# Attention in a hybrid encoder step: where VectorE combines the preceding tile, for tiles wider than 512 columns

## The chip, the cores and the metric

One core of a Trainium2 chip runs the whole step as one program. The metric is the device time of one execution in microseconds (us), lower is better. The median of three runs stands for the kernel; beside it there is one profiled execution with a trace of every instruction.

## The reference: what is computed

One layer of a streaming encoder: a modulated norm, an input projection, two mixers side by side (a state-space group and a differential-attention group), an output projection, and a gated convolutional feed-forward part. A prompt of 1,024 rows and eight samples of 16 rows (each with a cache of 512 keys) go through it. The change touches differential attention alone:

```python
def diff_attention(q, k, v, qpos, kpos, lam, rel_bias):
    s = jnp.einsum('bqhmd,bkhmd->bhmqk', q, k) * (DA_DK ** -0.5)       # m: two maps
    ...
    visible = (kpos[None, :] // CHUNK) <= (qpos[:, None] // CHUNK)
    p = jax.nn.softmax(jnp.where(visible, s + bias, -jnp.inf), axis=-1)
    attn = p[:, :, 0] - lam * p[:, :, 1]
    return jnp.einsum('bhqk,bkhd->bqhd', attn, v)
```

Each of four heads has two maps: two score matrices, each with a softmax of its own. The second is taken off the first with a factor, and the difference weighs the values.

## The kernel before, in words

**Tiles.** The prompt's attention is 32 tiles (4 heads, 8 blocks of 128 query rows). Block i sees (i + 1) x 128 key columns, so that its width is 128 to 1,024. In each head the blocks come in the order 7, 0, 6, 1, 5, 2, 4, 3 (`TILE_ORDER`), so blocks 7, 6, 5 and 4 are the ones wider than 512 columns (1,024, 896, 768 and 640). "Block 7" below is the tile of that block in some head; heads count from 0. The eight samples' tiles stand between them: ahead of the prompt tiles number 5, 9, 13, 17, 21, 25, 28 and 31 (`SAMPLE_BEHIND`). The list of the 40 is `WORK`, and w is a place in it.

**Work of one tile, over three engines.** TensorE (PE) makes the scores of both maps (L985). For each map VectorE (DVE) adds the bias to the last 256 columns (L1551) and takes the negated row maximum (L1552, `row_max`). ScalarE (ACT) makes the exponentials of that map and their sums (L2058). When both maps have theirs, VectorE combines them: a reciprocal (L1570), a factor (L1571), and one pass over the width that writes `attn` (L1576). This is `combine`; a sample's is `combine_s` (L1582 to L1591). TensorE turns `attn` in blocks of 128 (L650), in one piece of up to four blocks or, for a wide tile, in two pieces, ScalarE copies each piece out of PSUM (L2087, `attn_T`), and TensorE multiplies with the values (L1046); ScalarE copies the product into `o_T` (L2104). TensorE also turns the samples' cached keys (L650 with `k_cache`), and ScalarE copies them (L2074).

**Order.** Every engine runs a list that is written out by hand, step by step over w, and waits on semaphores. In step w VectorE did the two maxima of tile w and then combined tile w - 1. TensorE and ScalarE do this:

```python
# TensorE, step w (L1063)
scores(w)
attn_turn(w - 2, 0)
attn_values(w - 3)            # waits for ScalarE's last copy of tile w - 3
attn_turn(w - 2, 1)           # only where tile w - 2 is wide
# ScalarE, step w (L2106)
turn_out(w - 2, 0)
o_out(w - 3)
exps(w)                       # map 0, then map 1: each waits for its row maximum
turn_out(w - 2, 1)            # only where tile w - 2 is wide
```

(The two lists are shortened: the key turns and their copies stand ahead of `scores` and `turn_out`, and samples have functions of their own.) Two PSUM banks take turns for everything that TensorE turns and for the products with the values, so each use also waits until ScalarE has emptied the use two before it (`aux_free`).

Of the kernel before, what the change touches and what calls it, by code (L numbers as in the profile page):

```python
# [78 lines left out]
def build(nc, a, o):  # L79
# [231 lines left out]
    with ctx:  # L311
# [4 lines left out]
        def sem(name):  # L316
            if name not in sems:
                sems[name] = ctx.enter_context(nc.semaphore(name))
            return sems[name]
# [9 lines left out]
        def mark(ins, name):  # L329

            count[name] = count.get(name, 0) + 1
            ins.then_inc(sem(name), 1)
# [30 lines left out]
        def up_done(grp, u):  # L363

            if grp:
                return NUP0 + u + 1
            return max(i for i, (v, _) in enumerate(UP_ORDER) if v == u) + 1
# [5 lines left out]
        for i in range(LEAD, 2 * FT):  # L373
            for _ in range(2 if i == FT else 1):
                MIXED.append(("u", 1, sum(k == "u" for k, _, _ in MIXED)))
            MIXED.append(("d", 0, i))
        for i in range(FT):
            for _ in range(2 if i == 0 else 1):
                if sum(k == "u" for k, _, _ in MIXED) < 2 * FT:
                    MIXED.append(("u", 1, sum(k == "u" for k, _, _ in MIXED)))  # L380
            MIXED.append(("d", 1, i))
# [101 lines left out]
        WORK = []  # L483
# [3 lines left out]
        NW = len(WORK)  # L487
# [3 lines left out]
        def tile_width(w):  # L491

            kind, t = WORK[w]
            return (PROMPT[t][1] + 1) * P if kind == "p" else PAST + TS
# [15 lines left out]
        def score_bank(w, m):  # L510

            return 2 * PAIRS[w][m] if len(PAIRS[w]) == 2 else 2 * PAIRS[w][0] + m
# [41 lines left out]
        def aux_bank(of):  # L554

            return 6 + USE[of] % 2
# [654 lines left out]
        def _(ve):  # L1211
            def ch(ins):
                step(ve, ins, "dve_step")
# [143 lines left out]
            for c in range(8):  # L1357
# [11 lines left out]
                for t in range(4):  # L1369
                    w = SSMC[:, c, t:t + 1]  # L1370
# [168 lines left out]

            PSF = PS[:, :, :].rearrange("p b n -> p (b n)")  # L1540

            def row_max(w):
                t = WORK[w][1]
                W = tile_width(w)
                for m in range(2):
                    ve.wait_ge(sem("scores"), 2 * t + m + 1)
                    if t >= 2:
                        ve.wait_ge(sem("exp"), EXPS[PROMPT_AT[t - 2]][1])
                    c0 = 512 * score_bank(w, m)
                    near = PSF[:, c0 + max(0, W - 2 * P):c0 + W]  # L1550
                    ch(ve.tensor_tensor(near, near, BIASP[:, PROMPT[t][0], 2 * P - min(W, 2 * P):], ALU.add))  # L1551
                    mark(ve.tensor_reduce(MX[:, 2 * (t % 2) + m:2 * (t % 2) + m + 1], PSF[:, c0:c0 + W], AX.X,  # L1552
                                          ALU.max, negate=True), "row_max")
# [39 lines left out]
            def o_rows(w):  # L1593
                b = WORK[w][1]
                ve.wait_ge(sem("aux"), USE["values", w, 0] + 1)
                if b >= 1:
                    nxt = ("turn", w, 0)
                    ve.wait_ge(sem("aux"), USE[nxt] + 1)
                mark(ve.tensor_copy(OB[:, :], PS[:, aux_bank(("values", w, 0)), 0:P]), "o_rows")

            for w in range(NW + 3):
                if w < NW:
                    (row_max if WORK[w][0] == "p" else row_max_s)(w)
                if 1 <= w < NW + 1:
                    (combine if WORK[w - 1][0] == "p" else combine_s)(w - 1)
                if w == NW:
                    mark(ve.memset(EL[:, NH * NPT:], 0.0), "dve_step")
                    ch(ve.tensor_tensor(EL[:, 0:NH * NPT], L1[:, :], L1[:, :], ALU.mult))
                    ch(ve.tensor_scalar(EL[:, 0:NH * NPT], EL[:, 0:NH * NPT], -1.0, DV * EPS, ALU.add, ALU.mult))
                if w >= 3 and WORK[w - 3][0] == "s":  # L1610
                    o_rows(w - 3)
# [933 lines left out]
```

## Time and profile before

| | before |
|---|---|
| median of 3 runs | 1695.97 us (1694.97 to 1696.41) |
| the profiled execution | 1696.15 us, span 1694.4 us |
| PE busy over the span | 1593.2 us (94%) |
| DVE / ACT / POOL busy | 994.3 (59%) / 651.8 (38%) / 453.6 us (27%) |
| attention, 519 to 690 us of the span: PE / DVE / ACT busy | 144.9 / 123.9 / 105.9 us of 171 |

The profiled execution's time is its span and 1.75 us around it. Busy times are sums over instructions, and PE's ends are modelled. Attention is the stretch of the span from 519 to 690 us; there no engine is busy all the time, which is to say that each waits for the others in turn.

### The profile page before, as it was taken

The page shows a single profiled execution, that of the slowest core. Times are in us where ns is not written, and L with a number is a line of the kernel's source. Part 1 is how long each engine was busy: PE and PEld are TensorE (multiplying, and loading weights), DVE is VectorE, ACT ScalarE, POOL GpSimd, SP SyncE. Part 2 cuts the span into 40 slices and gives each one's busy share as a digit, 9 for nine tenths or more (in the row PEclk, how much of TensorE's full clock was granted, in tenths as well). Part 3 has the DMA queues.
Part 4 walks back from the last instruction along what each step waited for, and adds up shares of the span by engine and source line. Part 5 has one row for each costly group of instructions (what it writes and reads, how often), then busy time and mean ns, then how long its engine had stood idle before and what let it go on. Part 6 is the DMA issues. An engine that isn't in the chain of part 4 may idle for free.

```text
span 1694.4 us, 23175 instructions
## 1 busy us (share of the span) xinstructions
PE 1593.2 (94%) x9153; PEld 1412.9 (83%) x9153; DVE 994.3 (59%) x1603; ACT 651.8 (38%) x1143; POOL 453.6 (27%) x274
## 2 busy tenths in 40 slices
PE   4899998899998888789999999999999999999996
PEld 3689897689996666668899999999889989989875
DVE  3765416732115777654776666666466687667834
ACT  4531223321114666644332232224444454445532
POOL 0121124332201000365743333333621121112232
PEclk8899999899999999999999999999999999999998
DMA  9545110231214222327522222222364435544442
GB/s 326 198 163 199 38 28 1 57 89 38 67 53 155 101 101 77 124 87 205 203 68 67 66 62 63 63 78 73 99 188 124 133 103 167 160 135 122 149 164 70
DMA packets 163858, 189.09 MB, mean 112 GB/s; under 512 B 7851, under 2 KB 126868, under 8 KB 163731
## 3 DMA queue, kind: packets, MB, share of 16 engines
q1 hardware_dynamic: 148074, 148.89, 28.1%
q10 hardware_dynamic: 10300, 21.01, 4.1%
q0 software_dynamic: 5376, 17.71, 3.0%
q8 instruction: 73, 1.20, 0.3%
q14 instruction: 35, 0.28, 0.1%
HBM read 170.48 MB, written 17.11 MB: 111 GB/s over the span
## 4 chain that ended last, share of the span: by engine, by line
PE 81%; DVE 10%; ACT 3%; issue 3%; DMA 2%; POOL 1%; ACTq 0%; DVEq 0%; SPq 0%; POOLq 0%
PE PS L727 17%; PE PS L728 16%; PE PS L729 16%; PE PS L1188 4%; PE PS L1190 4%; PE PS L1189 4%; PE PS L650 4%; PE PS L1117 2%; PE PS L1118 2%; PE PS L1119 2%; PE PS L1046 2%; PE PS L985 2%; DVE y_new L1666 1%; PE PS L740 1%; DMA weights_raw<-in_w_up_dram 1%
## 5 line engine op out<-in xcount | busy, mean ns | idle before, releaser
L2347 POOL TENSOR_TENSOR weights_lo<-weights_raw,weights_hi 128x1024 fp32r<-128x1024 f32 x103 | 267.6, 2601 | 696.4 <-ACT weights_hi L1876 532.3
L727 PE MATMUL PS<-h_hi,weights_hi 128*128 128x384 f32 x1280 | 433.9, 339 | 3.3 <-DVE h_lo L1279 2.9
L728 PE MATMUL PS<-h_lo,weights_hi 128*128 128x384 f32 x1280 | 431.4, 337 | 0.0
L729 PE MATMUL PS<-h_hi,weights_lo 128*128 128x384 f32 x1280 | 431.3, 337 | 0.0
L1876 ACT ACTIVATE weights_hi<-weights_raw 128x1024 fp32r<-128x1024 f32 x202 | 213.2, 1058 | 159.1 <-PE PS L1190 97.5
L727 PEld LDWEIGHTS PS<-h_hi,weights_hi 128*128 128x128 f32 x1280 | 241.7, 189 | 11.9 <-issue 11.7
L728 PEld LDWEIGHTS PS<-h_lo,weights_hi 128*128 128x128 f32 x1280 | 241.7, 189 | 0.1
L729 PEld LDWEIGHTS PS<-h_hi,weights_lo 128*128 128x128 f32 x1280 | 241.6, 189 | 0.0
L1188 PE MATMUL PS<-weights_hi,g_hi 128*128 128x512 f32 x396 | 159.3, 402 | 8.9 <-POOL g_lo L2485 5.5
L1190 PE MATMUL PS<-weights_hi,g_lo 128*128 128x512 f32 x396 | 157.4, 397 | 0.0
L1189 PE MATMUL PS<-weights_lo,g_hi 128*128 128x512 f32 x396 | 156.6, 396 | 0.0
L2485 POOL TENSOR_TENSOR g_lo<-g_T,g_hi 128x384 fp32r<-128x384 f32 x54 | 70.4, 1305 | 271.5 <-ACT g_hi L2232 271.5
L1822 DVE TENSOR_TENSOR weights_lo<-weights_raw,weights_hi 128x1024 fp32r<-128x1024 f32 x99 | 121.7, 1256 | 21.2 <-ACT weights_hi L1876 18.6
L727 PE MATMUL PS<-h_hi_b,weights_hi 128*128 128x384 f32 x352 | 118.4, 336 | 0.2 <-DVE weights_lo L1822 0.2
L729 PE MATMUL PS<-h_hi_b,weights_lo 128*128 128x384 f32 x352 | 118.1, 336 | 0.0
L728 PE MATMUL PS<-h_lo_b,weights_hi 128*128 128x384 f32 x352 | 118.1, 336 | 0.0
L1188 PEld LDWEIGHTS PS<-weights_hi,g_hi 128*128 128x128 f32 x396 | 74.8, 189 | 26.4 <-DVE weights_lo L1822 7.9
L1190 PEld LDWEIGHTS PS<-weights_hi,g_lo 128*128 128x128 f32 x396 | 74.8, 189 | 18.6
L1189 PEld LDWEIGHTS PS<-weights_lo,g_hi 128*128 128x128 f32 x396 | 74.9, 189 | 15.7
L1733 DVE SCALAR_TENSOR_TENSOR beside_h_hi<-up_val,ffn_conv_cols,beside_h_hi 128x768 f32<-128x768 f32 x44 | 83.8, 1904 | 1.6
L1733 DVE SCALAR_TENSOR_TENSOR beside_h_hi<-up_gate,ffn_conv_cols,beside_h_hi 128x768 f32<-128x768 f32 x44 | 83.3, 1894 | 1.5
L2256 ACT ACTIVATE up_val<-PS 128x384 f32<-128x384 f32 x44 | 21.7, 492 | 138.1 <-PE PS L729 138.1
(389 smaller groups left out, 2465.3 us busy)
## 6 DMA issues: line engine op xcount, KB each, us to landing
weights_raw<-in_w_up_dram SPq DMA_DIRECT2D x88, 512.0 KB, 3.9
weights_raw<-in_w_down_dram SPq DMA_DIRECT2D x66, 512.0 KB, 4.4
w_ada_unit<-in_w_ada_dram SPq DMA_DIRECT2D x32, 512.0 KB, 5.4
weights_raw<-in_w_in_dram SPq DMA_DIRECT2D x24, 512.0 KB, 5.4
weights_raw<-in_w_out_dram SPq DMA_DIRECT2D x24, 512.0 KB, 4.0
w_ada<-in_w_ada_dram SPq DMA_DIRECT2D x4, 2048.0 KB, 16.7
k_cache<-in_cache_k_dram SPq DMA_DIRECT2D x8, 1024.0 KB, 7.7
v_cache<-in_cache_v_dram SPq DMA_DIRECT2D x8, 1024.0 KB, 5.5
```

The lines of the kernel that those rows point to most:

```text
L650: return pe.transpose(out, src, C("ident", rows, 0, rows))
L727: pe.matmul(out, wh, xh, start=(i == 0), stop=False)
L728: pe.matmul(out, wh, xl, start=False, stop=False)
L729: mm = pe.matmul(out, wl, xh, start=False, stop=(i == n - 1))
L1188: pe.matmul(out, GH[i % 2][:, lhs], WH[n % 3][:, ws], start=(f == 0), stop=False)
L1189: pe.matmul(out, GH[i % 2][:, lhs], WL[n % 3][:, ws], start=False, stop=False)
L1190: mm = pe.matmul(out, GL[i % 2][:, lhs], WH[n % 3][:, ws], start=False, stop=(f == FT - 1))
L1733: ins = ve.scalar_tensor_tensor(out=d, in0=src, scalar=w, in1=d, op0=ALU.mult, op1=ALU.add)
L1822: mark(ve.tensor_tensor(WL[n % 3][:, :], WR[:, n % 3, :], WH[n % 3][:, :].bitcast(F32), ALU.subtract), "w_lo_dve")
L1876: mark(ac.activation(WH[n % 3][:, :], WR[:, n % 3, :], ACT.Copy), "w_hi")
L2347: mark(gp.tensor_tensor(WL[n % 3][:, :], WR[:, n % 3, :], WH[n % 3][:, :].bitcast(F32), ALU.subtract), "w_lo")
L2485: mark(gp.tensor_tensor(GL[i % 2][:, :], GT[f][:, gg, :], GH[i % 2][:, :].bitcast(F32), ALU.subtract), "g_lo")
```

## The change

For a prompt tile w that is wider than 512 columns (and w at least 1), VectorE does the maximum of map 0, combines the tile before it, and then does the maximum of map 1. For all other tiles the order stays: both maxima, then the combination. Four wide tiles in each of four heads less the very first tile make 15 steps. No instruction is added or taken away, and the lists of the other engines stay as they were.

```diff
-            def row_max(w):
+            def row_max(w, maps=(0, 1)):
                 t = WORK[w][1]
                 W = tile_width(w)
-                for m in range(2):
+                for m in maps:
...
+            def combined(w):
+                (combine if WORK[w][0] == "p" else combine_s)(w)
+
             for w in range(NW + 3):
-                if w < NW:
-                    (row_max if WORK[w][0] == "p" else row_max_s)(w)
-                if 1 <= w < NW + 1:
-                    (combine if WORK[w - 1][0] == "p" else combine_s)(w - 1)
+                if 1 <= w < NW and WORK[w][0] == "p" and tile_width(w) > 512:
+                    row_max(w, (0,))
+                    combined(w - 1)
+                    row_max(w, (1,))
+                else:
+                    if w < NW:
+                        (row_max if WORK[w][0] == "p" else row_max_s)(w)
+                    if 1 <= w < NW + 1:
+                        combined(w - 1)
```

VectorE's list at block 7 of head 1, where the tile before it is block 3 of head 0 (512 wide) and a sample follows (L1560, L1563); lines with a minus stood there before, lines with a plus stand there now:

```order
 L1551 TENSOR_TENSOR PS<-PS,bias_prompt 128x256
 L1552 TENSOR_REDUCE row_max<-PS 128x1
-L1551 TENSOR_TENSOR PS<-PS,bias_prompt 128x256
-L1552 TENSOR_REDUCE row_max<-PS 128x1
 L1570 RECIPROCAL row_factor<-row_sum 128x1
 L1571 SCALAR_TENSOR_TENSOR row_factor<-row_sum_78,lambda_terms,row_factor 128x1
 L1576 SCALAR_TENSOR_TENSOR attn<-probs,row_factor 128x512
+L1551 TENSOR_TENSOR PS<-PS,bias_prompt 128x256
+L1552 TENSOR_REDUCE row_max<-PS 128x1
 L1560 TENSOR_TENSOR PS<-PS,bias_sample 128x144
 L1563 TENSOR_REDUCE row_max<-PS 128x1
```

The bias and the maximum of map 1 went behind the three instructions of the combination.

The same engine at block 5 of head 0, with block 1 (256 wide) before it:

```order
 L1551 TENSOR_TENSOR PS<-PS,bias_prompt 128x256
 L1552 TENSOR_REDUCE row_max<-PS 128x1
-L1551 TENSOR_TENSOR PS<-PS,bias_prompt 128x256
-L1552 TENSOR_REDUCE row_max<-PS 128x1
 L1570 RECIPROCAL row_factor<-row_sum 128x1
 L1571 SCALAR_TENSOR_TENSOR row_factor<-row_sum_78,lambda_terms,row_factor 128x1
 L1576 SCALAR_TENSOR_TENSOR attn<-probs,row_factor 128x256
+L1551 TENSOR_TENSOR PS<-PS,bias_prompt 128x256
+L1552 TENSOR_REDUCE row_max<-PS 128x1
 L1560 TENSOR_TENSOR PS<-PS,bias_sample 128x144
```

The same two instructions moved, behind a shorter combination.

## Rows read from the trace of the kernel before

**Rows 1.** Waits, 519 to 690 us: engine, line, releaser: us, times, longest.

```profile
PEld PS L650 <- DVE attn L1576: 13.2, 15, 1.8
...
PE PS L650 <- DVE attn L1576: 5.9, 5, 1.8
```

**Rows 2.** Timeline, block 7 of head 2: start, us, engine, instruction, idle before and releaser.

```profile
602.16 0.42 DVE L1551 TENSOR_TENSOR PS<-PS,bias_prompt 128x256 f32<-128x256 f32 x1
...
603.00 0.25 PE L996 MATMUL PS<-k_T,q_blocks 128*32 128x16 f32 x8
...
603.76 0.15 DVE L1570 RECIPROCAL row_factor<-row_sum 128x1 f32<-128x1 f32 x1
603.94 1.11 ACT L2058 ACTIVATE probs<-PS,row_max 128x1024 f32<-128x1024 f32 x1 [0.39 <-DVE row_max L1552]
...
604.87 0.31 DVE L1560 TENSOR_TENSOR PS<-PS,bias_sample 128x144 f32<-128x144 f32 x1
...
605.01 0.66 PE L650 MATMUL PS<-CONST,attn 128*128 128x128 f32 x4 [1.75 <-DVE attn L1576]
605.04 0.27 ACT L2087 ACTIVATE attn_T_a<-PS 128x128 f32<-128x128 f32 x1
...
605.50 0.30 PE L1046 MATMUL PS<-attn_T_a,v_rows 128*128 128x128 f32 x1
```

**Rows 3.** Timeline, block 5 of head 1.

```profile
583.23 0.15 DVE L1570 RECIPROCAL row_factor<-row_sum 128x1 f32<-128x1 f32 x1
...
584.08 0.31 DVE L1560 TENSOR_TENSOR PS<-PS,bias_sample 128x144 f32<-128x144 f32 x1
...
584.21 0.44 PE L650 MATMUL PS<-CONST,attn 128*128 128x128 f32 x2 [0.73 <-DVE attn L1576]
584.30 0.48 ACT L2087 ACTIVATE attn_T_a<-PS 128x384 f32<-128x384 f32 x1
...
584.92 0.35 PE L1046 MATMUL PS<-attn_T_a,v_rows 128*128 128x128 f32 x1 [0.27 <-ACT attn_T_a L2087]
```

**Rows 4.** Timeline, block 6 of head 0.

```profile
531.37 0.15 DVE L1570 RECIPROCAL row_factor<-row_sum 128x1 f32<-128x1 f32 x1
...
532.08 0.42 DVE L1551 TENSOR_TENSOR PS<-PS,bias_prompt 128x256 f32<-128x256 f32 x1
...
533.28 0.30 PE L650 MATMUL PS<-CONST,attn 128*128 128x128 f32 x1 [2.31 <-ACT attn_T_a L2087]
```

**Rows 5.** Timeline of head 3: block 7, then block 4.

```profile
646.69 0.63 PE L650 MATMUL PS<-CONST,attn 128*128 128x128 f32 x4 [1.52 <-ACT attn_T_a L2087]
...
676.99 0.15 DVE L1570 RECIPROCAL row_factor<-row_sum 128x1 f32<-128x1 f32 x1
...
677.96 0.37 ACT L2087 ACTIVATE attn_T_a<-PS 128x256 f32<-128x256 f32 x1
677.97 0.28 DVE L1599 COPY o_rows_s<-PS 128x128 f32<-128x128 f32 x1
...
678.76 0.28 PE L1046 MATMUL PS<-attn_T_a,v_rows 128*128 128x128 f32 x1
```

**Rows 6.** Timeline, block 4 of head 1.

```profile
593.19 0.82 DVE L1552 TENSOR_REDUCE row_max<-PS 128x1 f32<-128x640 f32 x1
...
595.20 0.80 ACT L2058 ACTIVATE probs<-PS,row_max 128x640 f32<-128x640 f32 x1
```

**Rows 7.** Timeline of PE: products with the values, and a wait behind attention.

```profile
533.77 3.38 PE L1046 MATMUL PS<-attn_T_a,v_rows 128*128 128x128 f32 x16 [0.19 <-ACT k_cache_T L2074]
...
613.51 1.95 PE L1046 MATMUL PS<-attn_T_a,v_rows 128*128 128x128 f32 x16
...
699.45 0.88 PE L1089 MATMUL PS<-o_squares,CONST 128*128 128x384 f32 x2 [2.80 <-DVE o_squares L1623]
```

**Rows 8.** Windows: stretch, length, PE busy (instructions), PEclk, DMA share, GB/s.

```profile
534.00:537.00 3.00, 3.00 (x17) 0.53 0.04 15
...
700.00:701.00 1.00, 1.00 (x9) 1.00 1.01 414
```

## The prediction

> **What bounds the kernel now.** I read the page first; by it TensorE is the busiest engine by far, so only what moves TensorE's work moves the time. The change touches attention alone, so the next view is the list of waits there. In it TensorE stands still 20 times for `attn`, the product of VectorE's combination: 13.2 us seen at the weight load and 5.9 us at the matmul itself, 19.1 us in all [rows 1]. That is the wait at which an earlier combination aims. But TensorE's list is in order, and what stands behind a removed wait decides whether the time comes back. So the third view is the timeline of TensorE, VectorE and ScalarE together at each of the 15 steps that the change reorders. There the reader is to see two chains out of one place on VectorE. One is the combination of tile w - 1, which TensorE's next turn waits for. The other is the maximum of map 1 of tile w; behind it ScalarE makes the exponentials of map 1, and only behind those, in ScalarE's own list, copies the second piece of tile w - 2, for which TensorE's product with the values waits. The change makes the first chain earlier and the second later.
>
> **Block 7 of heads 1 and 2.** Head 2 is the one shown; head 1 runs alike [rows 2]. The first instruction behind map 0's maximum starts at 602.16, the combination at 603.76: it moves up by 1.60 us. It holds VectorE until 604.87, that is 1.11 us, and by that much map 1's bias and maximum move back. On TensorE the sample's scores end at 603.25 (603.00 and 0.25). The turn that waited until 605.01 can start at 603.41 (605.01 less 1.60), so nearly all of the 1.75 us wait goes. The turn takes 0.49 us (605.01 to 605.50) and then ends at 603.90. The next instruction of TensorE is the product with the values of the older tile, at 605.50 before. It needs ScalarE's copy of 605.04, which took 0.27 us and directly followed the exponentials that started at 603.94, 0.39 us idle for the maximum of map 1. These all move by 1.11: the copy runs 606.15 to 606.42. From the end of such a copy to the product that waits for it are 0.14 us (584.30 and 0.48 make 584.78, the product starts at 584.92 [rows 3]). So the product starts at 606.56 in place of 605.50: **1.06 us later**, although the wait named in the profile is gone. The new wait is longer than the old one, and it is for ScalarE. Two heads: 2.12.
>
> **Block 5 of heads 0, 1 and 2.** Three steps of the same kind, with a combination of 256 columns; head 1 is shown [rows 3]. It holds VectorE from 583.23 to 584.08, 0.85 us. TensorE's wait of 0.73 for `attn` goes, but behind it the product already waits 0.27 for the copy of 584.30. All of the 0.85 arrives at the product: 3 x 0.85 = 2.55.
>
> **Block 6 of head 0.** Here tile w - 2 is block 7. The combination is of 128 columns, 531.37 to 532.08, 0.71 us, and TensorE's wait of 2.31 us is for ScalarE's copy already [rows 4]. Cost 0.71.
>
> **Head 3.** Its block 7 has the same combination, and the turn there waits for the copy directly (1.52, because a key turn stands between them in the two banks) [rows 5]: 1.11 us. Its block 4 has the wide block 5 at w - 2, unlike the other heads. The combination holds VectorE 0.98 us (676.99 to 677.97). The copy of 677.96 then ends at 679.31 (677.96, 0.98 and 0.37) and the product starts at 679.45 in place of 678.76: 0.69 us [rows 5].
>
> **The other seven steps.** In blocks 6 of heads 1 to 3 and blocks 4 of heads 0 to 2 tile w - 2 is a sample, so there is no second copy. The cover is ScalarE itself: its map 1 exponentials start only after those of map 0. At block 4 the maximum ended at 594.01 and the exponentials started at 595.20 [rows 6]; that is room of 1.19, against the 0.98 of the combination and a hand-over of some 0.14 us, taken from the one between ScalarE and TensorE above. I cost it at nothing; with the cover gone it would be 0.98. The combinations at block 6 are shorter (0.71). Block 5 of head 3 follows a sample; no second copy stands behind it, and I take nothing, with 0.85 as the upper bound.
>
> **Sum.** 2.12 + 2.55 + 0.71 + 1.11 + 0.69 = 7.18 us later. Nothing downstream gives it back: what TensorE waits for after each of these places (exponentials behind `o_T`, key copies) starts from its own products, so the shift is handed on to the end of attention, and the next stage starts from there.
>
> **The clock.** One term has no row of its own. At each of the three blocks 7 TensorE now stands still for some 2.66 us in one piece (603.90 to 606.56), 1.75 before. An idle stretch of 2.31 us [rows 4] was followed by a granted clock of 0.53 (the level of 1.2 GHz for nearly all of it) from 534 to 537 us; one of 2.80 us behind attention [rows 7] left the clock at 1.00 [rows 8]. So one of this length may or may not cost. The price of a fall is bounded by 16 products that took 3.38 us at the lower level and 1.95 at the upper [rows 7], 1.43 us. The lower end is no fall, the upper three, 4.3 us. I take one: 1.4.
>
> The profiled execution took 1696.15 us. With 7.2 and 1.4 that is 1704.75, and as the median of the runs is 0.18 below that execution, I say 1704.6.
>
> **Rivals.** *The gaps close (faster).* If the copy did not follow the exponentials, the turns' waits would simply go: 2 x 1.75 at block 7 and 3 x 0.73 at block 5, 5.7 us, so 1690.3. For it speaks that these are TensorE's own waits, named as such. Against it: the copy ends only 0.19 us before the product at block 7 (605.31 against 605.50) and after the turn at block 5, where the product waits for it in this profile. It decides at the place of the copy in ScalarE's list: it holds if the second copy runs before map 1's exponentials. The Trainium skill (Perfetto Trace Analysis, Identifying Performance Opportunities) advises to find the gaps on the busiest engine, see which semaphore ends them, and make that dependency start sooner; followed at its word it gives this rival's time, while here the trace has a second dependency right behind the first.
>
> *The delay is partly covered (no change).* If ScalarE had room, as at block 4, at the blocks 5 too, and the clock held, 7.18 less 2.55 would leave 4.6; if half of the remaining delay were also made up, some 2.3 us, 1698.3. For it: seven of 15 steps are covered. Against it: at block 5 ScalarE idles for the maximum of map 1, so there is no room.
>
> *The clock falls oftener (slower still).* Three falls and the uncovered steps at a few tenths each: 7.2 + 4.3 + 1 = 12.5, 1708.5.
>
> **How the numbers follow.** The forecast (all eight delays arrive, none to two falls: 1703.2 to 1706.1) has 0.75, the clock rival 0.10, the covered rival 0.09, the faster one 0.06. The range is 1700.0 to 1708.5: it takes in most of the clock rival and cases in which a third of the delay is covered. A difference of 0.2% (3.4 us) is about what a measurement of this kernel can tell. Of the covered rival's 0.09 I count 0.02 beyond that bound: faster 0.06, same 0.07, slower 0.87.
>
> **What would show it.** In the changed profile the waits of TensorE for `attn` should fall well below 19 us, while those of L1046 and L650 for ScalarE's `attn_T` grow by more. At block 7 TensorE's product should start 3.3 us after the sample's scores end (2.25 before, 603.25 to 605.50), and ScalarE's idle time for the row maximum should grow by about 1 us there. The period from one head's block 7 to the next should be about 1.9 us longer (1.06 and 0.85). It would be wrong if products follow turns without a gap, if the copies run ahead of the exponentials, or if TensorE's granted clock falls at each head.

## The result

The changed kernel took 1714.32 us (median of 4 runs, 1711.55 to 1716.68), the kernel before 1696.19 us beside it (4 runs, 1694.97 to 1697.39): ratio 1.0099, 95% interval 1.0087 to 1.0111, slower by 1%. In later runs, with more of the kernel before (63 in three lots), that one's medians were 1697.47, 1698.73 and 1698.18 us and single runs reached 1706.86; the changed kernel, run again with the last lot, had 1713.36 us and a ratio of 1.0088 (1.0070 to 1.0107). So the loss is 15 to 18 us. I had said 1704.6 us: the way was right, and 8.6 us of forecast loss are about half of the measured.

The profiled execution of the changed kernel took 1715.53 us. Its page, parts 1 and 2 (PEclk in 40 slices):

```profile
span 1713.7 us, 23175 instructions
## 1 busy us (share of the span) xinstructions
PE 1606.5 (94%) x9153; PEld 1424.2 (83%) x9153; DVE 998.1 (58%) x1603; ACT 652.3 (38%) x1143; POOL 454.4 (27%) x274
...
PEclk8899999899998999898999999999999999999998
```

The same instructions, a span longer by 19.3 us, and TensorE busy for 13.3 us more with the same matmuls. The same matmuls taking longer points at the clock, and the mean granted clock over the span is 0.969 here, 0.978 in the profile before.

The waits in attention (519 to 707 us; engine, line, releaser: us, times, longest), answering to [rows 1]; ScalarE's lines stand 8 further down in this kernel, so L2095 is the copy of L2087 and L2066 the exponentials of L2058:

```profile
ACT probs L2066 <- DVE row_max L1552: 17.8, 22, 3.7
PEld PS L1046 <- ACT attn_T_a L2095: 12.6, 6, 2.7
PE PS L1046 <- ACT attn_T_a L2095: 11.3, 6, 2.5
PE PS L650 <- ACT attn_T_a L2095: 8.5, 9, 3.0
...
PEld PS L650 <- DVE attn L1576: 0.5, 2, 0.3
...
PE PS L650 <- DVE attn L1576: 0.3, 2, 0.2
```

Two more lines of the profile before (519 to 690 us) belong beside these:

```profile
PE PS L650 <- ACT attn_T_a L2087: 6.7, 9, 2.3
...
PE PS L1046 <- ACT attn_T_a L2087: 0.5, 2, 0.3
```

The rows of the weight loads (PEld) and of the matmuls (PE) see the same stretches: ahead of the turn at block 7 of head 2 the matmul waited 1.75 us before [rows 2], and its weight load 1.85:

```profile
605.00 0.42 PEld L650 LDWEIGHTS PS<-CONST,attn 128*128 128x128 f32 x4 [1.85 <-DVE attn L1576]
```

So the two kinds must not be added, as the 19.1 us of the prediction are; it counts five stretches twice. By the matmul rows alone TensorE's wait for `attn` fell from 5.9 to 0.3 us. In its place six products with the values (L1046) wait 11.3 us for ScalarE's second copy, 0.5 before, and the turns (L650) wait 8.5 us for copies, 6.7 before. Together that is 7.0 us more waiting, so the list of waits itself says that the change costs.

The timeline at block 7 of head 2, answering to [rows 2]:

```profile
609.60 0.15 DVE L1570 RECIPROCAL row_factor<-row_sum 128x1 f32<-128x1 f32 x1
...
610.45 0.25 PE L996 MATMUL PS<-k_T,q_blocks 128*32 128x16 f32 x8
...
610.71 0.42 DVE L1551 TENSOR_TENSOR PS<-PS,bias_prompt 128x256 f32<-128x256 f32 x1
...
610.85 0.66 PE L650 MATMUL PS<-CONST,attn 128*128 128x128 f32 x4 [0.15 <-DVE attn L1576]
...
612.49 1.12 ACT L2066 ACTIVATE probs<-PS,row_max 128x1024 f32<-128x1024 f32 x1 [1.50 <-DVE row_max L1552]
...
613.60 0.27 ACT L2095 ACTIVATE attn_T_a<-PS 128x128 f32<-128x128 f32 x1
...
614.01 1.35 PE L1046 MATMUL PS<-attn_T_a,v_rows 128*128 128x128 f32 x9 [2.50 <-ACT attn_T_a L2095]
```

Read it from the sample's last scores (610.45). The turn follows them after 0.40 us (2.01 before, 603.00 to 605.01). The combination held VectorE for 1.11 us (609.60 to 610.71), ScalarE's idle time ahead of map 1 grew from 0.39 to 1.50, again 1.11, and the product starts 3.56 us after those scores, 2.50 before: 1.06 later, the forecast to the digit.

And the granted clock (PEclk is the number behind the bracket of counts) in some windows of TensorE:

```profile
546.00:550.00 4.00, 3.56 (x18) 0.59 0.00 0
570.00:574.00 4.00, 4.00 (x24) 0.58 0.02 4
615.00:618.00 3.00, 3.00 (x16) 0.50 0.00 0
660.00:663.00 3.00, 3.00 (x16) 0.53 0.00 0
673.00:676.00 3.00, 3.00 (x44) 0.51 0.02 5
701.00:703.00 2.00, 2.00 (x12) 0.50 0.00 0
711.00:720.00 9.00, 6.94 (x21) 0.50 0.84 332
```

0.50 is the level of 1.2 GHz. The first four stretches stand right behind the longer idle stretches at block 5 of head 0 and at blocks 7 of heads 1, 2 and 3, which end at 546.44, 569.66, 614.01 and 658.35. The profile before has two stretches at the lower level at the start of attention (524 to 527 us, and 534 to 537 [rows 8]), the changed one two like them (at 526 to 530 and 536 to 540 us). Behind 537.5 us the profile before has none in attention:

```profile
537.50:690.00 152.50, 131.39 (x1226) 1.00 0.27 91
```

**Where the 19.1 us went.** TensorE's last turn of attention starts at 706.81 (689.82 before); both profiles enter attention 0.26 apart (518.40 and 518.14), so attention took 16.7 us more. TensorE's list is the same in both, so one can follow how much later each instruction starts. At the eight places of the forecast this lag grows by 7.1 us, the delays (below). It grows by 8.4 us more over the six stretches at the lower clock that the profile before does not have: 1.64 us behind block 5 of head 0, 1.19, 1.19 and 1.14 behind the blocks 7, 1.58 at 673 and 1.62 at 701 us, some 1.4 us each. At block 7 of head 2, say, the product starts 8.51 us later (605.50 [rows 2] and 614.01), and the sixteen products behind the lower clock 9.70 us later (613.51 [rows 7]):

```profile
623.21 1.95 PE L1046 MATMUL PS<-attn_T_a,v_rows 128*128 128x128 f32 x16
```

The remaining 1.2 us arise mostly ahead of 540 us, where both profiles have their two stretches at the lower clock, at different work. Behind attention TensorE's first product of the output projection (L1117) stands at 721.21, 702.07 before: another 2.2 us, during 711 to 720 us at the lower clock.

### The profile page after: what moved, and what is told of

Its sections match the earlier page's. It is cut to its first block, busy times and chain, and to the rows that moved or that the text cites. A ratio compares the mean times of both kernels' runs of the same rounds, so it can differ in the third digit from the quotient of the medians.

```text
span 1713.7 us, 23175 instructions
## 1 busy us (share of the span) xinstructions
PE 1606.5 (94%) x9153; PEld 1424.2 (83%) x9153; DVE 998.1 (58%) x1603; ACT 652.3 (38%) x1143; POOL 454.4 (27%) x274
## 4 chain that ended last, share of the span: by engine, by line
PE 82%; DVE 10%; ACT 3%; issue 2%; POOL 1%; DMA 0%; ACTq 0%; DVEq 0%; SPq 0%; POOLq 0%
PE PS L727 17%; PE PS L728 16%; PE PS L729 16%; PE PS L1188 5%; PE PS L1190 5%; PE PS L1189 5%; PE PS L650 4%; PE PS L985 2%; PE PS L1046 2%; PE PS L1117 2%; PE PS L1118 2%; PE PS L1119 2%; DVE row_max L1552 1%; DVE y_new L1674 1%; PE PS L740 1%
```

## The experiments

Theory one: some 7 us are the handed-on delay of map 1, the rest is TensorE's clock, which falls behind the longer idle stretches. Rivals: the extra loss is more delay along the semaphores; or the combination between two maxima costs in itself.

One reading is common to all. Each run has a time and a mean granted clock. Over the 147 runs of all kernels here (the first four of the kernel before left out), with a mean of its own for each kernel in each lot, a line through the pairs has a slope of 1.03 us more for each 0.001 of clock less. With it each kernel's mean can be put at one clock, 0.976 (that of the runs before):

| kernel | median us | ratio, 95% interval | mean clock | us at clock 0.976, less before |
|---|---|---|---|---|
| before (63 runs, three lots) | 1697.47, 1698.73, 1698.18 | 1 | 0.976 | 0 (1698.56) |
| changed (4 and 5 runs) | 1714.32, 1713.36 | 1.0099, 1.0088 | 0.969 | +8.2 |
| idle stretches filled | 1705.48 | 1.0050 (1.0038 to 1.0063) | 0.976 | +7.2 |
| covered seven only | 1698.76 | 0.9997 (0.9983 to 1.0011) | 0.976 | -0.2 |
| copy between the maps | 1696.61 | 0.9999 (0.9988 to 1.0010) | 0.976 | -1.3 |
| old order, pass twice | 1704.30 | 1.0036 (1.0024 to 1.0048) | 0.972 | +1.5 |
| second-piece eight only | 1710.78 | 1.0073 (1.0054 to 1.0093) | 0.970 | +6.6 |
| blocks 5, copy moved | 1695.91 | 0.9984 (0.9969 to 0.9999) | 0.975 | -2.8 |
| copy moved alone | 1695.83 | 0.9986 (0.9972 to 0.9999) | 0.977 | -1.4 |
| blocks 5, all copies moved | 1696.12 | 0.9987 (0.9976 to 0.9998) | 0.977 | -2.3 |

The last column goes by means, not medians. It has an uncertainty of some 0.3 to 0.6 us from the scatter of the runs, and that of the slope (0.06) adds up to 0.4 us where the clock is far from 0.976. That falls of the clock in attention cost what a line through the scatter says is taken, not shown; the lag counted in the trace above is a second reading.

**Filling the idle stretches.** On TensorE, ahead of the turn:

```diff
+                if w >= 1 and w + 1 < NW and pieces(w + 1) == 2 and pieces(w - 1) == 2 and w + 2 not in KEY_STEPS:
+                    for _ in range(18 if tile_width(w + 1) == 1024 else 12):
+                        turn(PS[:, bank, 0:P], ATT[:, t % 2, 0:P])
```

> The changed kernel, with the first block of attn turned 12 or 18 times more (the same result written again) at five of the places where TensorE now waits for ScalarE's second copy: block 5 of heads 0 to 2 and block 7 of heads 1 and 2. Theory one (7.2 us of the loss are handed-on delay, the rest is TensorE's clock, which falls after the new idle stretches): the idle stretches of 1.93 and 2.50 us shrink below 0.6 us, the products start where they did, and three of the six additional falls (at 547, 571 and 615 us) are gone; at some 1.6 us each the time is near 1709.5 us, between 1706 and 1712. Rival (the extra loss is not the clock's: more delay along the chain of semaphores): the time stays at 1714 us or grows.

It took 1705.48 us, 8.8 us less than the changed kernel's first median, with 84 turns more (12 each at the blocks 5 of heads 0 to 2, 18 each at the blocks 7 of heads 1 and 2, and 12 at block 4 of head 3, which the edit's condition takes in too). The 1.6 us of the expectation for a fall came from sharing out all of attention's loss beyond the delays; by the lag above it is 1.4. The run's timeline at block 7 of head 2, and windows of the granted clock:

```profile
609.55 2.62 PE L650 MATMUL PS<-CONST,attn 128*128 128x128 f32 x22 [0.15 <-DVE attn L1579]
612.71 1.35 PE L1049 MATMUL PS<-attn_T_a,v_rows 128*128 128x128 f32 x10 [0.53 <-ACT attn_T_a L2098]
```

```profile
546.00:550.00 4.00, 3.39 (x31) 1.00 0.00 0
569.00:574.00 5.00, 4.30 (x34) 1.00 0.02 5
612.00:617.00 5.00, 4.28 (x36) 1.00 0.03 9
660.00:664.00 4.00, 4.00 (x29) 1.00 0.02 4
703.00:713.00 10.00, 5.95 (x33) 1.00 0.83 316
```

The product starts 3.56 us after the scores (609.15 to 612.71) as in the changed kernel, so the delay is untouched; what is gone is the lower clock. At equal clock this kernel is 7.2 us slower than the one before, about the delay by itself. The median came out just below the expected range of 1706 to 1712. The clock also held at places that were not filled (660 and 703 us) in the profiled execution, which took 1707.86 us: behind the wait of 2.64 us at block 7 of head 3 (to 655.90) it did not fall here.

**The covered steps.** The condition of the new order got `pieces(w - 2) == 1` added.

> The new order at the seven steps alone where tile w - 2 has no second piece (blocks 6 of heads 1 to 3, blocks 4 of heads 0 to 2, block 5 of head 3). Theory one: no new wait of TensorE, no new idle stretch, 1696 us, within 1 us of the kernel before. Rival (a combination between two maxima costs in itself, on VectorE or through ScalarE's later map 1): 0.7 to 1 us at each step, 1701 to 1703 us.

Ratio 0.9997, and 0.2 us less at equal clock. So seven of the 15 steps cost nothing that can be told (the interval ends at 1.9 us for all seven), and neither does a combination between two maxima in itself. The two first profiles say the same more sharply: at block 4 of head 1 TensorE's lag is 7.44 us ahead of it (586.56 and 594.00) and 7.45 behind (603.00 and 610.45). That rival falls.

**The others.** The same with `pieces(w - 2) == 2`.

> The new order at the eight steps alone where tile w - 2 has a second piece (blocks 5 of heads 0 to 2, blocks 7 of heads 1 to 3, block 6 of head 0, block 4 of head 3): what the run on the covered seven left out. Theory one: all of the loss is here, 7.2 us of delay and some 6 falls of the clock, 1714 us, between 1710 and 1717. Rival (the covered steps have a part in it): below 1710 us.

1710.78 us, 6.6 us more than before at equal clock, with a mean clock of 0.970: all of the loss is at these eight steps, within the intervals of the two ratios.

**The copy between the maps.** On ScalarE, in the changed kernel:

```diff
             for m in range(2):
...
+                    if m == 0 and copy_early(w):
+                        turn_out(w - 2, 1)
...
-                if 2 <= w < NW + 2 and pieces(w - 2) == 2:
+                if 2 <= w < NW + 2 and pieces(w - 2) == 2 and not copy_early(w):
                     turn_out(w - 2, 1)
```

(`copy_early(w)` holds at the eight steps.)

> The changed kernel, with ScalarE's copy of the second piece of tile w - 2 moved between the exponentials of map 0 and those of map 1 at the eight steps that have both. If the copy's place behind map 1 makes the loss (theory one), the products start right behind the turns: about 1.0 us gained at each of three blocks 5 against the kernel before, next to nothing at blocks 7, where the combination of block 7 itself comes next; 1693.5 us, between 1692 and 1698 if the clock falls once or twice. Rival (VectorE's reordering itself, or the later exponentials of map 1, make the loss): above 1705 us.

Ratio 0.9999: the whole loss is gone with one copy moved ahead of one exponential in ScalarE's list, at the eight steps. The rival, above 1705 us, falls. TensorE's timeline at block 5 of head 1, then at block 7 of heads 2 and 3:

```profile
581.36 0.44 PE L650 MATMUL PS<-CONST,attn 128*128 128x128 f32 x2
...
581.64 1.61 PE L1046 MATMUL PS<-attn_T_a,v_rows 128*128 128x128 f32 x13
```

```profile
600.49 0.66 PE L650 MATMUL PS<-CONST,attn 128*128 128x128 f32 x4 [0.15 <-DVE attn L1576]
600.99 1.30 PE L1046 MATMUL PS<-attn_T_a,v_rows 128*128 128x128 f32 x10
603.97 0.63 PE L650 MATMUL PS<-CONST,k_cache 128*128 128x128 f32 x4 [1.68 <-ACT attn_T_b L2100]
...
644.40 1.75 PE L1046 MATMUL PS<-attn_T_a,v_rows 128*128 128x128 f32 x10 [2.37 <-ACT k_cache_T L2087]
```

The products now follow the turns. But at the blocks 7 the wait comes back one instruction later (1.68 us for the other copy, or 2.37 us at head 3 for the key copy), both behind the same late exponentials on ScalarE. Behind the 2.37 us the clock fell once:

```profile
644.00:648.00 4.00, 3.60 (x20) 0.65 0.00 0
```

In this profile only the blocks 5 keep their gain, and the kernel ends where the one before was, inside the expected range but not at its 1693.5.

**An idle stretch without any reordering.** The kernel before, with the pass that writes `attn` done twice for the tile ahead of three blocks 7:

```diff
+                if w + 1 < NW and WORK[w + 1][0] == "p" and tile_width(w + 1) == 1024:
+                    ch(ve.scalar_tensor_tensor(out=ATT[:, q, 0:W], in0=PR[:, q, 1, 0:W], scalar=RL[:, q:q + 1],
+                                               in1=PR[:, q, 0, 0:W], op0=ALU.mult, op1=ALU.add))
```

> The kernel before in its old order, with the pass that writes attn done twice for the tile ahead of blocks 7 of heads 1 to 3 (the same result). TensorE's idle stretch there grows by about 0.8 us, from 1.75 to some 2.5 us, and nothing else is reordered. Delay alone (rival): 0.8 us at each of two or three places, 1697.6 to 1698.4 us. With falls of the clock after idle stretches of this length (theory one): up to three falls of some 1.6 us more, 1699.5 to 1703 us, and a lower granted clock behind these places in the profile.

1704.30 us against 1697.47, by the ratio some 6 us for 2 us of delay, and above the expected range of 1699.5 to 1703. TensorE at block 7 of head 1 (the products behind it also in the profile before), and the clock behind the blocks 7 of heads 1 and 2:

```profile
563.86 1.12 PE L650 MATMUL PS<-CONST,attn 128*128 128x128 f32 x4 [2.54 <-DVE attn L1579]
564.77 2.34 PE L1046 MATMUL PS<-attn_T_a,v_rows 128*128 128x128 f32 x10
```

```profile
564.26 1.31 PE L1046 MATMUL PS<-attn_T_a,v_rows 128*128 128x128 f32 x10
```

```profile
564.00:567.00 3.00, 3.00 (x15) 0.50 0.04 13
608.00:611.00 3.00, 3.00 (x16) 0.52 0.00 0
```

The wait is 2.54 in place of 1.75 us, and the ten products behind it take 2.34 us, where they took 1.31 us in the profile before. At block 7 of head 3 the wait was 1.86 us, and the clock held. So a longer idle stretch brings the lower clock without any reordering, at two of three places in this profile. By the mean clock (0.972) 3.7 us of the 5.2 by which the means differ are the clock's, and 1.5 remain at equal clock.

**The blocks 5 alone.** New order and moved copy at blocks 5 of heads 0 to 2, old order elsewhere.

> The new order at blocks 5 of heads 0 to 2 alone, with ScalarE's second copy between the maps there: the three steps at which the run with the moved copy gained 0.8 us each. Theory one: 2.4 us off the kernel before run on the same chip (1697.5 us there so far), 1695 us, and no longer idle stretch of TensorE than before, so no additional falls of the clock. Rival (the gain is eaten by the combination of block 5, which comes later): no change, 1697.5 us or more.

Ratio 0.9984 (0.9969 to 0.9999), 2.8 us less at equal clock: a version that is faster than both kernels, by 0.16%, with an interval that just leaves out no change. The profile agrees: from the first turn to the last (518.35 to 687.39) attention takes 169.04 us, 171.68 in the profile before (518.14 to 689.82), and both have two stretches at the lower clock in it, at its start.

**The copy moved alone**, in the kernel before, with VectorE's old order:

> The kernel before with VectorE's old order, and only ScalarE's second copy between the maps at the same eight steps. Theory one: it takes away the waits for the copy alone: 0.27 us at each of three blocks 5, about 0.4 us at block 7 of head 3, up to 1 us at block 6 of head 0; 1695.5 to 1697 us against 1697.5 us. Rival (the copy's move was what made the run with the moved copy equal to before, and the reordering still costs): 5 us or more below the kernel before.

Ratio 0.9986 (0.9972 to 0.9999). The rival's 5 us are not there; the waits for the copy were worth 1.4 us at equal clock. The ratio is that of the blocks 5 version within both intervals, so it is not shown that VectorE's new order adds anything to the moved copy.

**Both together.**

> The new order at blocks 5 of heads 0 to 2 alone, and ScalarE's second copy between the maps at all eight steps that have one. If the gains found apart add up: 2.4 us from the blocks 5 and about 1 us more from block 6 of head 0 and block 7 of head 3, so 3.4 us (0.2%) below the kernel before on the same chip. If they overlap, or if the moved copy at the blocks 7 costs as much as it gives: 2.4 us, as in the run with the blocks 5 alone.

Ratio 0.9987 (0.9976 to 0.9998): no more than the blocks 5 alone. The gains do not add up, as far as 12 runs can tell.

**The changed kernel again.**

> The changed kernel again, on one chip with more runs of the kernel before. Theory one: 7 to 9 us slower at equal mean granted clock, and a mean clock lower by some 0.006, which with 1.07 us for each 0.001 (the slope over the runs so far) makes 6 us more: 13 to 16 us in all. Rival (the clock follows no order and only varies from run to run): the mean clock is that of the kernel before within 0.001, and the difference is 7 to 9 us.

1713.36 us, 15.2 us more than the kernel before beside it, with a mean clock of 0.969 against 0.976: as expected, and the rival, by which the clock only varies from run to run, falls. The windows of its profile show the lower clock behind the same four places, and behind attention:

```profile
548.00:550.00 2.00, 2.00 (x12) 0.50 0.00 0
572.00:574.00 2.00, 2.00 (x11) 0.50 0.00 0
616.00:618.00 2.00, 2.00 (x11) 0.50 0.00 0
661.00:663.00 2.00, 2.00 (x11) 0.50 0.00 0
708.00:718.00 10.00, 7.85 (x24) 0.50 0.78 306
```

So four of the six additional stretches within attention come with the change each time; those at 673 and 701 us were in the first profile alone; the second has the two at the start of attention longer instead.

## Why the prediction was wrong in size

**The chains: right.** The forecast's two chains out of one place on VectorE are what the profile shows. TensorE's wait for `attn` went (5.9 to 0.3 us on the matmul rows; no term of the sum rests on the 19.1), the wait for the second copy came, and moving that copy in the changed kernel took the whole loss away. The signs came too: at block 7 the product starts 3.31 us after the sample's scores end (3.3 forecast; 610.45 and 0.25, to 614.01).

**The delays: right, place by place.** Block 7 of head 2: 1.06 forecast, 1.06 measured. Block 5 of head 0: 2.55 us from the sample's last scores to the product in the new profile, where the old one had 1.69 at the same place (542.06 to 543.75), so 0.86 for the forecast 0.85. The first two lines are of the new profile, the others of the old:

```profile
543.89 0.25 PE L996 MATMUL PS<-k_T,q_blocks 128*32 128x16 f32 x8
...
546.44 3.05 PE L1046 MATMUL PS<-attn_T_a,v_rows 128*128 128x128 f32 x14 [1.93 <-ACT attn_T_a L2095]
```

```profile
542.06 0.25 PE L996 MATMUL PS<-k_T,q_blocks 128*32 128x16 f32 x8
...
543.75 1.80 PE L1046 MATMUL PS<-attn_T_a,v_rows 128*128 128x128 f32 x14 [0.28 <-ACT attn_T_a L2087]
```

(The same fourteen products take 3.05 us in place of 1.80: the lower clock behind the wait.)

Block 6 of head 0: the wait is 2.95 us, 2.31 before, 0.64 for 0.71. Block 7 of head 3: 2.64 for 1.52, 1.12 for 1.11. Block 4 of head 3: 1.06 us between the turn of 693.00 and the product of 694.06, 0.36 before (678.40 to 678.76), 0.70 for 0.69. With two more blocks 5 and one more block 7 like those, 7.1 us against 7.18. The seven steps that I costed at nothing cost nothing that can be told (second experiment). The filled kernel's 7.2 us at equal clock say the same; the changed kernel's 8.2 lie 1 us higher, which the uncertainty of that column can hold but doesn't explain. The shift was also handed on, as forecast: nothing in attention gave it back.

**The clock: the step that failed.** "I take one: 1.4." The bounds had been none to three falls, 0 to 4.3 us, at the three blocks 7. The price of a fall was right (1.1 to 1.6 us, 1.4 on average, against 1.43); the number was wrong, six in place of one, 8.4 us in place of 1.4. Taking one of three had no row behind it: I looked at the three longest new idle stretches (2.66 us forecast; 2.50, 2.50 and 2.64 measured) and took them for coins, and the clock fell behind them three times of three in both profiles of the changed kernel. The stretch at block 5 of head 0, which I had not counted among them, was followed by the lower clock as well, though the forecast's own terms there (waits of 0.73 and 0.27 us and the 0.85) make one idle stretch of some 1.85 us; it measured 1.93. The stretches at 673 and 701 us stand behind waits of 1.60 and 1.41 us that the kernel before has too (1.59 and 1.41), with no fall there in its profile. That the clock falls at each head had been named as a sign of being wrong, and it came. It shows in the period from one block 7 to the next, 41.24 us before (564.26 to 605.50) and 44.35 now (569.66 to 614.01):

```profile
569.66 1.59 PE L1046 MATMUL PS<-attn_T_a,v_rows 128*128 128x128 f32 x10 [2.50 <-ACT attn_T_a L2095]
```

That is 3.11 us longer in place of the forecast 1.9, and 1.2 of it is one fall. In all the mean clock went from 0.976 to 0.969, and 0.0067 at 1.03 us for each 0.001 are 6.9 us; with the 8.2 at equal clock that makes the 15.1 us by which the changed kernel stands above the later runs of before.

**The base of the sum.** The first four runs of the kernel before lay 1.3 to 2.5 us below the medians of the later 63. The profile that I summed from had a clock of 0.978, at the better end of that kernel's runs (0.971 to 0.979), so the sum started from a good draw.

**What stays open.** The length of the idle stretch does not by itself say whether the clock falls. 1.93 us was followed by the lower clock at head 0's block 5 and not at those of heads 1 and 2 (1.93 us too); 2.64 us at block 7 of head 3 was, in both profiles of the changed kernel, and was not in the filled one; 1.60 and 1.41 us were in one profile. What decides it was not tried. Nor is it shown that the change brings the stretch behind attention (711 to 720 us): the blocks 5 version shows it too (its line follows), and so does the kernel with the moved copy alone, with VectorE in its old order.

```profile
692.00:701.00 9.00, 6.90 (x19) 0.50 0.80 309
```

## What to carry to other kernels

When an instruction is pulled ahead on one engine, what it is pulled ahead of goes back by its whole duration; follow that second chain through the other engines' lists to the next instruction of the engine that waits, before counting the removed wait as a gain. Where TensorE sits between two waits, removing the first can just lengthen the second, as here, and what was two short idle stretches with a little work between becomes one long one; price it with the clock rows of the same profile, and count every new stretch of that length rather than one. A list of waits is read on one track, since weight loads and matmuls show the same stretch twice. The remedy was on the third engine: one copy moved ahead of an exponential that it did not need to wait for. That move without any reordering on VectorE (ratio 0.9986) does as well as the best version with it (0.9984).

## What the runs showed of the hardware

In attention, where TensorE also waits, each of six stretches at the lower clock made it 1.1 to 1.6 us later. Over all runs 0.001 less of the mean granted clock goes with 1.03 us more of the whole time, where 0.001 of the 1,700 us span are 1.7 us, so about 60% of it shows in the time. The same kernel's runs differ along with it: 63 runs of the kernel before, 1694.3 to 1706.9 us, with mean clocks from 0.979 down to 0.971. Turns of a block already turned, with no use but to fill a wait, were worth 8.8 us of 1,714.
